# First stage: filter tables ahead of x, both filter spectra ahead of the second modulation chunk, first chunk's halves between the norm's blocks

## The reference

```python
x = x + sincos_2d(x.shape[1])
sh1, sc1, ... = adaln(c, ada_w[l], ada_b[l])        # silu(c) @ ada_w + ada_b, in 6 parts
h = modulate(rms_norm(x, norm1_g[l]), sh1, sc1)     # then h @ w_in
...
h = sin(fr1 * (z @ w1 + b1))                        # hyena_filters: a small network
h = sin(fr2 * (h @ w2 + b2))
h = (h @ w3).reshape(L, 2, HY_WIDTH) * exp(-t * deltas)[:, None, :]
kern = concatenate([h_fwd, zeros, flip(h_bwd[1:])])
y = irfft(rfft(u, n=2L) * rfft(kern))               # the filter's spectrum: rfft(kern)
```

## Time and profile before

| | us |
|---|---|
| median of three runs | 1970.4 |
| the profiled execution, its own time | 1971.46 |
| span of the profiled execution | 1969.6 |
| PE busy in the span | 1868.5 |
| DVE, ACT, POOL busy | 818.2, 586.1, 387.5 |

### The profile page before, as it was taken

The page is one execution under the profiler, slowest core; times in us unless marked ns, Lnnn a source line. Parts: engine busy times, 40 slices in busy tenths (PEclk is TensorE's granted clock), DMA queues, the critical chain, the costliest instruction groups (busy, mean ns, idle before and its releaser), DMA issues.

```text
span 1969.6 us, 26164 instructions
## 1 busy us (share of the span) xinstructions
PE 1868.5 (95%) x11248; PEld 1366.6 (69%) x11248; DVE 818.2 (42%) x1342; ACT 586.1 (30%) x892; POOL 387.5 (20%) x205
## 2 busy tenths in 40 slices
PE   5999999999999999999999899999999899889998
PEld 2777796964444343447887657888888688679998
DVE  1615255731111111116343744566655625574333
ACT  2513103331111111113113535223333411544554
POOL 2000000120000000004003132333443210425665
PEclk8999999989999999999999899999999899999999
DMA  9479917669999999992224004454445222414451
GB/s 357 153 256 344 341 44 278 215 270 429 426 427 428 427 427 427 427 394 82 86 86 161 3 33 171 150 181 162 149 150 182 92 91 89 171 47 168 174 196 38
DMA packets 111425, 429.84 MB, mean 218 GB/s; under 512 B 5706, under 2 KB 8821, under 8 KB 98512
## 3 DMA queue, kind: packets, MB, share of 16 engines
q1 hardware_dynamic: 109056, 416.56, 54.5%
q0 software_dynamic: 2256, 11.62, 1.6%
HBM read 427.11 MB, written 1.05 MB: 217 GB/s over the span
## 4 chain that ended last, share of the span: by engine, by line
PE 65%; DMA 17%; DVE 5%; PEld 5%; issue 3%; ACT 3%; POOL 2%; PEldq 0%; SPq 0%; POOLq 0%; DVEq 0%; ACTq 0%
PE bank L556 64%; DMA ring<-in_moe_w_down 7%; PEld bank L556 4%; DMA H<-in_moe_w_down 4%; DMA arena<-in_moe_w_down 4%; DMA ring<-in_ada_w 2%; PE bank L571 1%; PEldq L535 0%; POOL arena L1889 0%; POOL arena L1888 0%; DVE H L1976 0%; DMA ring<-in_w_in 0%; DVE H_low L1983 0%; POOL arena L1893 0%; POOL arena L1891 0%
## 5 line engine op out<-in xcount | busy, mean ns | idle before, releaser
L556 PE MATMUL bank<-arena_r 128*128 128x256 f32 (+1 forms) x2176 | 591.7, 339 | 12.1 <-ACT arena_r L1380 6.1
L556 PE MATMUL bank<-arena_r,ring_low 128*128 128x512 f32 (+2 forms) x1920 | 596.4, 342 | 1.8 <-DVE H_low L1983 1.0
L556 PEld LDWEIGHTS bank<-arena_r 128*128 128x128 f32 x2176 | 384.9, 190 | 63.2 <-issue 18.2
L556 PE MATMUL bank<-arena 128*128 128x64 bf16 (+8 forms) x2908 | 366.1, 319 | 42.7 <-DMA arena<-in_hy_filt_w 11.7
L556 PEld LDWEIGHTS bank<-arena_r,ring_low 128*128 128x128 f32 (+1 forms) x1920 | 352.5, 188 | 47.7 <-issue 2.7
L556 PEld LDWEIGHTS bank<-arena 128*128 128x128 bf16 (+4 forms) x2908 | 206.2, 132 | 203.8 <-issue 168.6
L556 PE MATMUL bank<-H_low,arena_r 128*128 128x512 f32 (+1 forms) x672 | 217.3, 340 | 0.0
L556 PE MATMUL bank<-ring,arena 128*64 128x512 f32 x768 | 172.0, 603 | 8.4 <-DMA ring<-in_moe_w_down 7.9
L2556 DVE SCALAR_TENSOR_TENSOR X<-bank,mod,X 128x256 f32<-128x256 f32 x216 | 94.2, 478 | 196.6 <-PE bank L556 196.6
L1915 POOL TENSOR_TENSOR ring_low<-ring,arena_r 128x2048 fp32r<-128x2048 f32 x31 | 142.3, 4614 | 131.1 <-DVE ring_low L2568 69.1
L1394 ACT ACTIVATE arena<-bank 128x512 f32<-128x512 f32 (+2 forms) x106 | 51.2, 496 | 368.5 <-PE bank L556 368.5
(11 more groups left out here) (304 smaller groups left out, 1845.4 us busy)
## 6 DMA issues: line engine op xcount, KB each, us to landing
ring<-in_w_mlp SPq DMA_DIRECT2D x32, 2048.0 KB, 7.8
ring<-in_w_in SPq DMA_DIRECT2D x26, 2048.0 KB, 9.1
ring<-in_ada_w SPq DMA_DIRECT2D x24, 2048.0 KB, 11.6
ring<-in_moe_w_up SPq DMA_DIRECT2D x17, 2048.0 KB, 23.2
ring<-in_moe_w_gate SPq DMA_DIRECT2D x17, 2048.0 KB, 27.8
arena<-in_moe_w_up SPq DMA_DIRECT2D x15, 2048.0 KB, 22.4
ring<-in_moe_w_down SPq DMA_DIRECT2D x14, 2048.0 KB, 23.3
arena<-in_moe_w_down SPq DMA_DIRECT2D x13, 2048.0 KB, 24.3
```

The lines of the kernel that those rows point to most:

```text
L556: ins = nc.tensor.matmul(o, l, r, start=start, stop=stop, skip_group_check=True)
```

## The change

The table `hy` is issued ahead of x, pos and ctx. On PE both filter products and both spectra stand ahead of the second modulation chunk, and the sums come between that chunk's product and its turn; chunks two and three are multiplied one behind the other, and their turns follow. The decayed filters have a buffer for each direction (`f_nats`). DVE takes the decay products ahead of the add to x. ACT copies the spectra behind the squares and ahead of the first row copy. The high halves of the first `w_in` chunk stand on ACT ahead of the shifts and behind the first of them; the low halves stand on DVE inside `norm`, ahead of its blocks 1 and 4.

```diff
-        f_nat = A3(21632, 2, 512)
+        f_nats = [A3(21632, 2, 512), A3(4096, 2, 512)]
+        f_nat = f_nats[0]
...
             filters(0)
+            pe.wait_ge(S("filt_dec"), 1)
+            filters(1)
+            for d in range(2):
+                spectrum(d)
             ada(1, 1, 7, blk=0)
             flush()
-            spectrum(0)
+            sums(0, 1, 2 * L, 1)
             ada_turn(1, 7, 1)
-            sums(0, 1, 2 * L, 1)
             ada(2, 2, 6, blk=0)
             flush()
-            pe.wait_ge(S("rms_ready"), 1)
-            filters(1)
-            ada_turn(2, 6, 0)
             ada(3, 3, 7, blk=0)
             flush()
+            ada_turn(2, 6, 0)
             ada_turn(3, 7, 1)
-            spectrum(1)
...
                 square(k, 2 * L).then_inc(S("squares"), 1)
+            for ft in range(4):
+                act.wait_ge(S("filt_mm"), 4 + ft + 1)
+                A_(KS[:, ft, :], ps[(0, 3, 5, 4)[ft]][:, :], ACT.Copy).then_inc(S("filt_sin"), 1)
...
+            act.wait_ge(full[win(0) % RING], arrived(win(0)))
+            first_high(0)
             for k in range(KT):
...
-                if k == 3:
-                    for ft in range(4):
-                        act.wait_ge(S("filt_mm"), 4 + ft + 1)
-                        A_(KS[:, ft, :], ps[(0, 3, 5, 4)[ft]][:, :], ACT.Copy).then_inc(S("filt_sin"), 1)
+                if k == 0:
+                    first_high(1)
...
+            bring(A(15360, 4096), T["hy"], "tables_in")
             bring(X[:, :, 0:L], tall(T["x"]), "x_in")
             bring(A3(0, KT, L), tall(T["pos"]), "x_in")
             bring(X[:, :, L:2 * L], tall(T["ctx"]), "x_in")
-            bring(A(15360, 4096), T["hy"], "tables_in")
...
+            take_chunk(0, 0, 6, 0)
+            dve.wait_ge(S("tables_in"), 16)
+            for d in range(2):
+                decayed(d)
             dve.wait_ge(S("x_in"), 16 * 3)
...
-            norm(0, 0, 0, (0, 1), True, RS0, Hp)
+            norm(0, 0, 0, (0, 1), True, RS0, Hp, {1: lambda: first_low(0), 4: lambda: first_low(1)})
```

More of the change, by code:

```diff
@@ L637, in spectrum @@
                         tab = f_fw if d == 0 else f_tab.rearrange("p (a b) -> p a b", a=2)
-                        mm(o, tab[:, tb, ft * P:(ft + 1) * P], f_nat[:, tb, :], d == 0 and tb == 0, d == 1 and tb == 1,
+                        mm(o, tab[:, tb, ft * P:(ft + 1) * P], f_nats[d][:, tb, :], d == 0 and tb == 0, d == 1 and tb == 1,
                            inc="filt_mm" if d and tb else None)
@@ L1420, in _, with first_high @@
             ada_rows(2, 6, 0)
-            n = win(0)
-            act.wait_ge(full[n % RING], arrived(n))
-            for a in range(2):
+            ada_rows(3, 7, 1)
+            def first_high(a):
                 s = slice(2048 * a, 2048 * (a + 1))
-                A_(W0h[0][:, s], slot(n)[:, s], ACT.Copy).then_inc(S("high_copied"), 1)
-            ada_rows(3, 7, 1)
+                A_(W0h[0][:, s], slot(win(0))[:, s], ACT.Copy).then_inc(S("high_copied"), 1)
+            act.wait_ge(full[win(0) % RING], arrived(win(0)))
+            first_high(0)
             for k in range(KT):
@@ L1984, in low_half, with norm @@
                                               ALU.add, ALU.subtract)
-            def norm(call, b, which, halves, split=True, root=RS, high=Hh):
+            def norm(call, b, which, halves, split=True, root=RS, high=Hh, between={}):
                 dve.wait_ge(S("rms_ready"), call + 1)
                 for k in range(KT + 1):
+                    if k in between:
+                        between[k]()
                     if k < KT:
@@ L2025, in _, with decayed @@
                 V.tensor_scalar(a, a, 3.1415925, -3.1415925, ALU.min, ALU.max).then_inc(S("filt_arg"), 1)
+            def decayed(d):
+                dve.wait_ge(S("filt_mm"), 2 + d + 1)
+                for tb in range(2):
+                    i = V.tensor_tensor(f_nats[d][:, tb, :], f_dec[:, tb, :], ps[1 + tb][:, :], ALU.mult)
+                i.then_inc(S("filt_dec"), 1)
+            take_chunk(0, 0, 6, 0)
+            dve.wait_ge(S("tables_in"), 16)
+            for d in range(2):
+                decayed(d)
             dve.wait_ge(S("x_in"), 16 * 3)
@@ L2028, in _ @@
                 V.tensor_tensor(X[:, 4 * a:4 * a + 4, 0:L], X[:, 4 * a:4 * a + 4, 0:L], A3(1024 * a, 4, L), ALU.add).then_inc(S("x_added"), 1)
[L2030 to L2034, removed]
             def split_first(j):
@@ L2040, in split_first, with first_low @@
                 V.tensor_tensor(low(n), slot(n), W0h[j % 2].bitcast(F32), ALU.subtract).then_inc(S("w_split"), 1)
[L2042 to L2049, removed]
+            def first_low(a):
+                n = win(0)
                 s = slice(2048 * a, 2048 * (a + 1))
@@ L2052, in _ @@
                 V.tensor_tensor(low(n)[:, s], slot(n)[:, s], W0h[0][:, s].bitcast(F32), ALU.subtract).then_inc(S("w_split"), 1)
-            take_chunk(0, 3, 7, 12)
+            for g in range(1, 4):
+                take_chunk(0, g, 6 + g % 2, 4 * g)
             dve.wait_ge(S("base_in"), 16)
```

## The result

The changed kernel is slower: its median is 1979.72 us (1978.02 to 1986.26, 7 runs), the kernel before had 1971.44 in the same comparison (1968.82 to 1976.21, 7 runs); ratio 1.0042, interval 1.0031 to 1.0054. That is +8.3 us. Forecast were +4.1, with 1971.0 to 1978.5 as the range: the sign is right, the size is half.

A forecast was written before the change was run, and what follows sets the result against it. PE, busy 95% of the span, bounds the kernel. Norm 1.5 us later, halves +4.5, DVE stalls of 1.4 gone: +4.6, of which +4.1 reaches PE, giving 1974.5 us; range 1971.0 to 1978.5.

The forecast's parts named there:

- The table crowds the first chunk: First stage: the table's 16 KB packets slow the first modulation chunk, landing it 2.4 us later; bounds 0 and 3.2.
- The first rival: First chunk's load: no crowding by the table, all 2.4 us earlier, +1.7 in sum, 1972.1 us; chance 0.27.
- PE's level until it rises: Filter products and spectra: PE's clock low until 4.8 us after the second filter product starts, then high; spectra end at 46.4.
- the 11.7 from there to the last turn: PE from the spectra's end: remaining modulation chunks, sums and turns at the high level take 11.7 us, ending at 58.1.
- The halves inside the norm: DVE's norm: two low halves add 4.5 us, so the seventh block is done 16.4 us after the start.
- The clock after the hole before the tiles: First tile pair: low clock after PE's idle 58.1 to 63.3; 14 us of it gives +7.3, 1977.7; chance 0.13.
- the rival's arithmetic: First tile pair: a low-clock stretch of 4 us costs nothing; it begins to cost when it outlasts some 9 us.
- What is hidden: Adds to x and sums covered by the spectra; loads behind the late second slot and DVE's next-chunk work covered too.
- PE's order decides, faster: First tile pair: products held by PE alone, so 4.4 us come back, 1966.0 us; chance 0.06.

The follow-up runs named there:

- e1: Changed kernel, but POOL issues the table only when the first modulation chunk has landed; ratio 1.0021 to the kernel before, median +4.3 us.
- e5: Changed kernel with the table issued behind x, pos and ctx again, new PE and DVE order kept; ratio 1.0048 to the kernel before.
- e2: Changed kernel with the first chunk's high and low halves ahead of the norm; ratio 1.0011 to the kernel before, median +3.3 us.
- e0: Changed kernel once more, unaltered; 1979.46 us against 1972.43 for the kernel before, ratio 1.0034.
- e3: Changed kernel with the table waiting for the first chunk and the halves ahead of the norm; 1975.42 us against 1974.97 before, ratio 1.0005.
- e4: Kernel before with only the halves moved inside the norm; ratio 1.0021, median +5.1 us.
- e7: Changed kernel with the table waiting for the first chunk and products of a zeroed tile in PE's holes; ratio 1.0026 to the kernel before.
- e9: Kernel before with only products of a zeroed tile added in PE's holes; 1978.9 us, ratio 1.0032.
- e10: Kernel before, unaltered, profiled a second time; ratio 1.0010 against itself, interval 0.9994 to 1.0026.
- e8: Changed kernel with products of a zeroed tile in PE's holes and the halves ahead of the norm; ratio 1.0039 to the kernel before.

## Why the prediction was wrong, by its own steps

- *The table crowds the first chunk.* Right as a mechanism (e1 and e5 each remove it by another way), mis-sized: 3.0 to 3.5 us against the 13.77 of before instead of 2.4, above the bound of 3.2 in two of three executions (17.23, 17.15 in e2, 16.73 in e0). The first rival, packets of at most 4096 bytes by the Trainium skill ("DMA: Bandwidth & Descriptors", section "SWDGE vs HWDGE vs iDMA"), is refuted a second time by 0.75 MB in 46 packets.
- *PE's level until it rises: the step that failed.* I took the level high from 4.8 us after the second filter product's start and bounded it by 5.9. It rose 8.9 us after it (30.27 to 39.2), in e0 7.8 (29.18 to 37.0), in e1 9.0 (25.23 to 34.2), in e3 and e5 9.3; only in e2 it was 6.4. Besides, the second filter layer and the turn ran at the low level in the profiled execution, as 1.10 and 1.86, which I had priced at the high one by leaving their rows as they were. My reading of the trace of before was wrong there: I had PE at the low level from its first products on and the granted clock at 0.50 until 37. The rows of 0.64 and 1.02 show the high level from 17.4, and the clock column reads 1.00 before it falls at 20.4. The bound came from two places where PE resumed after a hole of the kernel before. Even in the old order the rise scatters, 3.5 us after the second chunk's product starts in e4 and 5.9 in the trace that I had. Why it is later in the new order is open: e0 and e1 had some 3 us at the high level ahead of it, as the kernel before had, and it was late in them too. Of the +4.2 by which the norm's start missed (62.80 against 58.6), 1.1 are the chunk, 0.9 the steps up to the spectra and 2.0 the spectra (50.46 - 33.97 = 16.5 against 14.45); the 11.7 from there to the last turn were 11.8. These 4.2 on top of the forecast's +4.1 are the 8.3 by which the tile pair ends late. In e0 the miss was 2.6, of which the chunk had 0.6, the steps 0.3 and the spectra 1.5.
- *The halves inside the norm.* Right, in mechanism and size: 16.37 from the norm's start to the seventh block against 16.4; e2 prices their place at 3.8.
- *The clock after the hole before the tiles.* The level fell at 63.0 and was back at 73.3, and PE's first products, from 68.1 on, were 0.43 apart. It cost next to nothing (the pair ended 0.2 later than DVE's chain gives), as the rival's arithmetic had it for a short stretch.
- *What is hidden.* The adds to x and the sums were hidden (e7 shows where that ends: PE's sums at 45). The loads behind the late second slot were too: DVE took up the next chunk at 81.16, 0.19 us behind its own last step (near 77 forecast, 88 the limit).
- *PE's order decides, faster*: refuted, since PE waited 5.24 us for H_low before its first tile product.

## What to carry to other kernels

A transfer with large packets moved ahead on one queue is paid for by the other queue: before moving it, count the bytes that something is already waiting for, and let it go only when these have landed (e1, 2.8 us better in the median than e0). Work moved from an idle stretch of an engine into the loop that feeds the bottleneck costs its full time less the bottleneck's lag in that loop (3.8 of 4.5 us in the new order, an estimated 1.7 in the old one, where PE came later), even when its new place lets the loop begin earlier. Where a stage begins at the low level, two places of one trace don't bound the moment of its rise: state the sum with the whole stretch at the low level too, and read the level from the distance between products.

## What the runs showed of the hardware

The granted clock's column says 1.00 until its first entry, whatever the level: up to 63 us in the changed kernel's profile, while products were 0.86 apart until 38.4. Three profiled executions of six of the changed order (the changed kernel, e0, e1, e2, e3, e5) had their first entry in the column only behind 58 us. In the scan, 230 to 305 us, nine of the fourteen profiled executions had one to three stretches at the low clock of 3.4 to 10.3 us, among PE work of many small products with pauses under 1 us. One of 10.2 us adds 5 us to 208 instructions in the chain shown above. Three of the five that had none ran the order of before (before, e9, e10), the other two were e0 and e8, so chance isn't excluded either way. In the scan they make 10 us between the two profiled executions of the changed kernel, and they are why single executions were compared by their mark and not by their time.
